# Expert rows of 8 KB with one gather per pick, and weights laid out load by load, in a two-block transformer kernel on one core

## What is computed

```
q       = h @ w_q                            # h: normed token, 1024 wide
scores  = q against two sets of 128 sub-keys, the best 16 sums kept per head
gate    = softmax over the 16 scores of a head
for each of the 128 picks e of a token:
    a   = gelu( sum_d h[d] * U[e, d] )       # U, V: 16384 rows of 1024 float32 per layer
    y  += gate * a * V[e, :]
x       = x + y
```

## Time and profile before

| | |
|---|---|
| median of 3 runs | 2161.14 us |
| span of the profiled execution | 2111.6 us |
| TensorE matmul busy | 1648.0 us (78%) |
| VectorE busy | 1375.4 us (65%) |
| ScalarE busy | 388.8 us (18%) |
| GpSimd busy (gathers) | 1128.4 us (53%) |
| moved by DMA | 720.79 MB, mean 341 GB/s |
| of that by GpSimd's queue, by SyncE's | 536.94 MB, 182.85 MB |

### The profile page before, as it was taken

How to read it: one execution, slowest core, us unless ns; L and a number is a source line. 1 busy time by engine, 2 the same in 40 slices (tenths; PEclk the granted TensorE clock), 3 DMA queues, 4 the chain that set the end, 5 groups by cost and what they waited for, 6 DMA issues and landing times.

```text
span 2111.6 us, 15758 instructions
## 1 busy us (share of the span) xinstructions
PE 1648.0 (78%) x4610; PEld 828.8 (39%) x4610; DVE 1375.4 (65%) x3269; ACT 388.8 (18%) x902; POOL 1128.4 (53%) x1028
## 2 busy tenths in 40 slices
PE   3997999998567978987876888878768996555565
PEld 1465887444233434432343433333434442111111
DVE  6564432142796695687757668776784887777775
ACT  1022000012121222222122222221322221100001
POOL 0000000000377577577766767776687777777773
PEclk9977999998789979999796999999788999887667
DMA  9851569162799999999999999999999999999997
GB/s 357 303 197 60 165 194 329 57 238 80 245 372 385 401 399 407 401 406 380 400 396 406 404 403 406 408 397 401 397 354 384 407 394 365 408 409 409 409 410 313
DMA packets 254483, 720.79 MB, mean 341 GB/s; under 512 B 24518, under 2 KB 49598, under 8 KB 253886
## 3 DMA queue, kind: packets, MB, share of 16 engines
q0 software_dynamic: 147456, 536.94, 65.0%
q1 hardware_dynamic: 106942, 182.85, 24.2%
HBM read 718.66 MB, written 1.05 MB: 341 GB/s over the span
## 4 chain that ended last, share of the span: by engine, by line
PE 40%; DMA 21%; POOL 17%; DVE 13%; issue 7%; ACT 2%; SPq 0%; POOLq 0%; DVEq 0%; ACTq 0%
POOL gring L1699 17%; DMA gring<-in_peer_v_dram,sel_idx 17%; PE PS L621 13%; PE PS L753 7%; PE PS L825 5%; PE PS L826 5%; DVE gring L1537 4%; PE PS L727 4%; PE PS L566 3%; DMA gring<-in_peer_u_dram,sel_idx 2%; DMA wring<-in_hyb_w_in_dram 1%; DVE xs L1556 1%; PE PS L670 1%; PE PS L687 1%; PE PS L706 1%
## 5 line engine op out<-in xcount | busy, mean ns | idle before, releaser
L1699 POOL DMA_INDIRECT gring<-in_peer_u_dram,sel_idx x512 | 566.0, 1105 | 725.1 <-DVE sel_g L1523 556.2
L825 PE MATMUL PS<-gring,diags 128*128 128x512 f32 x736 | 449.0, 695 | 321.3 <-DMA gring<-in_peer_v_dram,sel_idx 211.5
L1699 POOL DMA_INDIRECT gring<-in_peer_v_dram,sel_idx x512 | 562.2, 1098 | 230.3 <-issue 130.5
L1537 DVE CUSTOM_DVE_ANT_0 gring<-gring,hs 128x1024 f32<-128x1024 f32 x400 | 482.1, 1221 | 134.3 <-DMA gring<-in_peer_u_dram,sel_idx 133.1
L826 PE MATMUL PS<-gring,diags 128*128 128x512 f32 x736 | 434.2, 676 | 0.0
L621 PE MATMUL PS<-wring,hTs 128*128 128x512 f32 (+3 forms) x968 | 410.4, 574 | 9.8 <-DVE hTs L1125 4.3
L825 PEld LDWEIGHTS PS<-gring,diags 128*128 128x128 f32 x736 | 135.4, 210 | 545.4 <-issue 383.4
L621 PEld LDWEIGHTS PS<-wring,hTs 128*128 128x128 f32 x968 | 179.8, 195 | 219.8 <-issue 217.4
L826 PEld LDWEIGHTS PS<-gring,diags 128*128 128x128 f32 x736 | 158.8, 216 | 210.5 <-issue 210.5
L1063 ACT ACTIVATE diags<-consts,acts 128x128 f32<-128x128 f32 x368 | 136.4, 397 | 511.3 <-PE PS L826 476.8
L1537 DVE CUSTOM_DVE_ANT_0 gring<-gring,PS 128x1024 f32<-128x1024 f32 x112 | 136.4, 1220 | 70.4 <-DMA gring<-in_peer_u_dram,sel_idx 70.4
(11 more groups left out here) (194 smaller groups left out, 1188.9 us busy)
## 6 DMA issues: line engine op xcount, KB each, us to landing
wring<-in_peer_w_q_dram SPq DMA_DIRECT2D x32, 1024.0 KB, 14.7
wring<-in_w_ada_dram SPq DMA_DIRECT2D x24, 1024.0 KB, 9.7
wring<-in_w_up_dram SPq DMA_DIRECT2D x44, 512.0 KB, 5.1
wring<-in_hyb_w_in_dram SPq DMA_DIRECT2D x20, 1024.0 KB, 8.3
wring<-in_w_in_dram SPq DMA_DIRECT2D x10, 1024.0 KB, 8.1
wring<-in_hyb_w_out_dram SPq DMA_DIRECT2D x8, 1024.0 KB, 19.2
gring<-in_peer_u_dram,sel_idx POOLq DMA_INDIRECT x512, 12.9
gring<-in_peer_v_dram,sel_idx POOLq DMA_INDIRECT x512, 13.4
```

Source lines behind the costliest of these rows:

```text
L825: pe.e.matmul(ybank[0], d, row[i % NG][:, 0:512], start=first, stop=last)
L1537: e.tensor_tensor_reduce(row[i % NG], row[i % NG], hbank if (l, t) == (1, 1) and hd else h[t], 1.0, 0.0, ALU.mult, ALU.add, acts[:, c:c + ...
L1699: gp.e.indirect_dma_start(out=row[i % NG], out_offset=None, in_=table, in_offset=bass.IndirectOffsetOnAxis(ap=sel_idx[:, c:c + 1], axis=0) ...
```

## The change

- **Tables.** U and V of an expert stand side by side in one row of 8 KB (`peer_uv`, made on the host), and one gather per pick brings both: 512 gathers of 1 MB where there were 1024 of 512 KB. The slot is kept until the pick's sum or addition is done.
- **Rings.** `NG` is 11 slots of 8 KB (22 columns of 4 KB where there were 16), `NW` is 4 where it was 6. The three late gain vectors share one buffer, `late`, which is loaded three times, and some vectors of the first block move.
- **Order of expert steps.** The `v` step of a pick follows the `u` step of the pick two later (`LAG` = 2).
- **Gates pick by pick.** ScalarE applies Gelu to one column when its dot is done, and multiplies it with the gate (a Copy with scale); then, in the `v` step, it builds the diagonal of the pick two earlier, no longer ahead. VectorE's multiplication by the gates is gone.
- **Weights.** The host lays out each load as 128 runs of 8 KB. A load is one DMA of one run per partition (four runs for the narrow columns). The `up` loads are one DMA each where they were two of 512 KB; the sub-keys are laid out the same way.

```diff
-NG = 16
-NW = 6
+NG = 11
+NW = 4
+ROW = 2 * D
+LAG = 2
...
+    for n in range(len(picks) + LAG):
+        step = []
+        if n < len(picks):
+            if picks[n] == (1, 1, 1, 0):
+                step.append(("hold",))
+            step.append(("u", *picks[n]))
+        if n >= LAG:
+            step.append(("v", *picks[n - LAG]))
+        experts.append(step)
...
-    together(16 + 32 * 7, PACE[0], c00, hybrid(1), choose(1, 0))
+    together(16 * 8 - 4, PACE[0], c00, hybrid(1), choose(1, 0))
...
-                loads += [(("up", s[1], g), 2) for g in range(2)]
+                loads += [(("up", s[1], g), 1) for g in range(2)]
...
-            def gate(l, t, hd):
-                c0 = 128 * t + 16 * hd
-                ac.wait_ge(dotted, 16 * round_n[(l, t, hd)])
-                ac.e.activation(acts[:, c0:c0 + 16], acts[:, c0:c0 + 16], ACT.Gelu).then_inc(act_done, 1)
+            def gate(l, t, hd, j):
+                c = 128 * t + 16 * hd + j
+                n = dot_n[(l, t, hd, j)]
+                ac.wait_ge(dotted, n)
+                ac.e.activation(acts[:, c:c + 1], acts[:, c:c + 1], ACT.Gelu).then_inc(act_done, 1)
+                ac.wait_ge(chosen, chosen_n[(t, l, hd // 2)])
+                ac.wait_ge(act_done, n)
+                ac.e.activation(acts[:, c:c + 1], acts[:, c:c + 1], ACT.Copy,
+                                scale=sel_g[:, c:c + 1]).then_inc(weighted, 1)
...
-                ac.wait_ge(weighted, round_n[(l, t, hd)])
+                ac.wait_ge(weighted, dot_n[(l, t, hd, j)])
...
-                for col, w, r0, nk, c0, n in parts:
-                    src = w[r0:r0 + 128 * nk, c0:c0 + n].rearrange("(k p) n -> p k n", p=128)
-                    sp.e.dma_start(slot[s][:, 0:nk, col:col + n], src).then_inc(w_landed[s], 16)
+                w, at, nk, n = places[unit]
+                src = a[w][l, at:at + 128 * nk * n].rearrange("(p c) -> p c", p=128)
+                if n == 512:
+                    sp.e.dma_start(flat[s][:, 0:nk * n], src).then_inc(w_landed[s], 16)
...
-                sp.e.dma_start(kv, a["peer_sub_keys_2"][l].rearrange("h t n c -> n (h t) c")).then_inc(w_landed[s], 16)
+                sp.e.dma_start(kv, a["peer_sub_keys_2"][l]).then_inc(w_landed[s], 16)
...
-                gp.e.indirect_dma_start(out=row[i % NG], out_offset=None, in_=table,
+                gp.e.indirect_dma_start(out=gring[:, ROW * (i % NG):ROW * (i % NG + 1)], out_offset=None, in_=table,
                                         in_offset=bass.IndirectOffsetOnAxis(ap=sel_idx[:, c:c + 1], axis=0)
                                         ).then_inc(row_landed[i % NG], 16)
```

More of the change, by code:

```diff
@@ L228, in order @@
     left = []
+    picks = [(*r, j) for r in ROUNDS for j in range(16)]
     experts = []
-    waiting = []
-    for now, past in zip(ROUNDS + [None], [None] + ROUNDS):
-        if now == (1, 1, 1):
-            waiting = waiting + [("hold",)]
-        for j in range(16):
-            if now:
-                experts.append(waiting + [("u", *now, j)])
-                waiting = []
-            if past:
-                experts.append(waiting + [("v", *past, j)])
-                waiting = []
-        if now:
-            waiting = [("gate", *now)]
+    for n in range(len(picks) + LAG):
[7 more added lines that the diff above has]
+        experts.append(step)
     at = [0]
@@ L310, in program @@
         hTs = sb("hTs", 8 * 256)
-        gains = sb("gains", 3 * D)
+        late = sb("late", D)
         tabs = sb("tabs", 4 * 112)
@@ L362, in program @@
         hT = hTs[:, :].rearrange("p (k s) -> p k s", k=8)
-        late = [gains[:, D * i:D * (i + 1)] for i in range(3)]
         norm_cols = small[:, 368:392]
@@ L435, in program @@
         chosen_n = {key: n // 7 for key, n in chosen_n.items()}
-        gather_n = {s: n - 1 for s, n in counted(("u", "v")).items()}
-        gathers = [s for s in steps if s[0] in "uv"]
         dot_n = {s[1:]: n for s, n in counted(("u",)).items()}
+        picks = list(dot_n)
         sum_n = {s[1:]: n for n, s in enumerate((s for s in steps if s[0] == "v" and not by_vector(*s[1:])), 1)}
@@ L1569, in vector_engine @@
                    "angles": angles, "score": score, "value": value, "fold": fold, "up": up, "gfold": gfold,
-                   "index": index, "mrope": mrope, "hold": hold, "u": dot, "gate": gate, "v": expert, "pick": pick}
+                   "index": index, "mrope": mrope, "hold": hold, "u": dot, "v": expert, "pick": pick}
             first = {"mod": modulate, "turn": attturn, "lin": mrope_key}
@@ L1580, in sync_engine, with weights @@
             sp = Lane(eng)
-            def weights(key, parts):
+            places = unit_places()
+            def weights(key, unit, l=0):
                 s, _ = w_at[key]
@@ L1639, in up @@
                     for g in range(2):
[L1640 to L1646 removed]
+                        weights(("up", ch, g), ("up", ch, g))
             def down(t, c, k):
```

161 lines of the change are left out of this document (89 added, 72 removed).

## The result

The changed kernel takes 2304.12 us (median of 4 runs, 2302.51 to 2309.47), the kernel before 2156.47 in the runs beside it: a ratio of 1.0677, 95% interval 1.0635 to 1.072 (the ratios here are taken over all runs and differ by 0.1% or so from the quotient of two medians). On the three chips of the experiments the kernel before takes 2113 to 2118 us, and the changed one, run again on one of them, 2304.8, ratio 1.0896 (1.0866 to 1.0927). The changed kernel is slower by 7 to 9%. The prediction was 2147, about the same as before, with a range up to 2235: it was wrong in the direction and outside its range.

What follows compares the result with a forecast made beforehand. From about 557 us the DMA engines were taken as the bound, with compute engines waiting for rows. Steps 1 to 5, -90 + 46 + 16 + 12 + 2 = -14, gave 2097.6 us of span, scaled to 2147; range 2080 to 2235.

Steps and rivals of the forecast that it cites:

- Step 2: Attentions of the mixed stretch: sums wait behind the newest dot, a ring through three engines; +46 us, range 0 to 68.
- the absorption: Before each attention phase the slot ring runs empty, so 8 rows go in stock; 117 of 136 loads still move.
- the length of the ring: Score-to-score time through TensorE, VectorE and ScalarE: 9.5, 8.8, 7.1 or 3.6 us a unit, 335 us for three attentions.
- Step 1: Gathers and weights from 557 us on: 8 KB runs move at 425 GB/s, 1443 us where 1533 stood, -90 us.
- second rival: Gathers don't move faster in runs of 8 KB: only -43 us in step 1, 2195 us; chance 0.15.
- Step 3: First block's feed-forward: with four weight slots, second loads of chunks 2 to 5 stall TensorE; +16 us.
- Step 4: Windows where VectorE is nearly always busy, some 200 us, can't follow faster DMA: +12 us (0 to 25).
- third rival: The same ring closes in the selection of experts too: +68 us, 2217 us; chance 0.18.
- Step 5: End of the kernel: after the last row come a dot, Gelu, gate and addition; +2 us.
- The scaling: Forecast span of 2097.6 us times 2161.14 / 2111.6 = 1.0235, giving 2147 us for the runs.
- Slower by over 2%: Measured time over 2204 us: chance 0.23, of which 0.17 from the third rival and 0.06 from the second.

Runs made afterwards that it cites:

- mending the attentions alone: Changed kernel with ScalarE building the diagonal right behind its gate only for the 91 picks between units of the three mixed-stretch attentions: 2120.2 us, ratio 1.0022.
- the two kernels above: The changed kernel (2304.12 us), and the changed kernel with ScalarE building each pick's diagonal right behind its own gate (2080.96 us).
- the repaired kernel: Changed kernel with ScalarE building each pick's diagonal right behind its own Gelu and gate, not two picks later: 2080.96 us, ratio 0.9849.
- the fastest kernel: Changed kernel with each diagonal right behind its gate, plus six slots instead of four for the first block's weight loads: 2062.32 us, ratio 0.9739.

## Why the prediction was wrong

The forecast of the span was 2111.6 - 90 + 46 + 16 + 12 + 2 = 2097.6. It was 2300.7.

**Step 2, the lag of two picks: right mechanism, wrong size. This is the step that failed.** It said +46 us; the place of the diagonal costs 224, 185 of them through the attentions. Two parts of its working fell.

The first, and larger, is the absorption. "As the ring runs empty before each phase, 8 rows to put in stock" supposes that before each attention the engines wait for rows. They don't: between 577 and 1800 us of the changed kernel VectorE's waits are these (engine, tile and line, releaser: us in all, times, longest):

```profile
DVE work L1374 <- PE PS L710: 180.2, 41, 7.5
...
DVE gring L1574 <- DMA gring<-in_peer_uv_dram,sel_idx: 14.8, 11, 2.6
```

14.8 us for rows, 180.2 for scores behind sums. In the kernel before it is 131.2 us for rows of U, in 96 waits, and 33.2 for scores: the ring did run empty there, and the step carried that over. The slots are taken when the first attention begins, and GpSimd waits for one to be released (108.8 of the 188 us before the first attention, for sums): by the trace 58 gathers have been issued by 765 us, and 47 picks summed or added, eleven apart. A full ring can't take more rows in stock; each is issued when a sum ends, and while TensorE waits, none is. The argument took from the kernel before that its DMA share is 1.02 everywhere, and so that the DMA engines would still be the bound between the attentions. Once the sums wait for the newest dot there too, they are not. The right account for a ring that nothing drains is the time of the phase less what its own picks and weights need: by the prediction's own numbers 136 loads' time less 81 picks and 12 loads of weights, 43 x 2.47 = 106 us where it had 46. In the attention windows 164 were measured, and mending the attentions alone gave back 185.

The second is the length of the ring. 335 us were forecast for the 45 intervals and 362.7 measured (139.6, 102.8 and 120.4 for 128, 98 and 109). A unit with dot, addition, dot and sum was to take 8.8 us; the one shown takes 10.2. From the end of a score to the start of the next sum it is 0.7 (803.84 to the Exp at 804.53) + 4.85 (Exp to sum) = 5.5 us, where 4.7 + 1.0 was worked out. It is the sum that is longer: 799.18 to 802.97 us, 3.8 where 2.4 was put in, a mean over all granted clocks, with 2.9 as the slow end. A TensorE that waits nearly 5 us before each sum is granted a clock of 0.65 between 765 and 835 us, and its passes take 1.14 us instead of 0.592 (rows of the two kernels above), about twice as long, as at the lower of its two levels, 1.2 GHz. The wait makes the sum longer, and the sum the wait. The gates' 0.29 and the diagonal's 0.39 us for the 0.21 and 0.33 of the text are small beside it.

**Step 1, longer runs: the rate was right, the reason for it incomplete.** 421 GB/s in pure gathers where 425 was taken, and 421 in the attention windows of the repaired kernel. The prediction's second rival, that gathers don't move faster in 8 KB, falls. The Trainium skill, "DMA: Bandwidth & Descriptors", section "SWDGE vs HWDGE vs iDMA", says that a packet is preferably at most 4096 B; no loss by it shows in this trace, where rows of 8192 B, with half the packets, moved at 421 GB/s and rows of 4096 B at 410. What the step had wrong is "GpSimd is just ahead of them". It took the 0.94 us of one gather of the pure stretch for the mixed one, where the kernel with only its weights changed shows 1.16. So in the kernel before GpSimd and the DMA engines were about even, GpSimd issuing nearly without a pause (907 of 1024 gathers). That the weights' part is worth nothing (2118.69 for 2112.86) and that two gathers instead of one cost 56 us both fit that, and neither could be seen in a sum of bytes and rates. Of the -90 the fastest kernel keeps some 50: its gathers start at 558.8 us, within 3 us of before, and its span is 2063.0 for 2111.6.

**Step 3, a ring of four for the weights: right in place, near in size, and the size in part by luck.** Four idle times of TensorE at the line of `up`, ended by loads of `w_up`, were forecast with 16 us in all. They are there, with 2.2 to 3.1 us each and 11.4 in all. The first gather starts 21 us later (577.5 for 556.2), and undoing the ring of four gives back 19. What fills the gap was in no term: from 235 to 320 us, where the four waits lie, TensorE is granted a clock of 0.92 for 1.00 before, and its matmuls of `up` are busy 162.3 us in all, against 155.5 in the fastest kernel, with six slots:

```profile
PE PS L793 <- DMA wring<-in_w_up_dram: 11.4, 4, 3.1
POOL gring L1724 <- DVE sel_g L1559: 577.5, 1, 577.5
```

**Step 4, stretches that can't follow, and the third rival.** +12 us were put down. The windows between the attentions lose 85 us, and the repaired kernel loses next to nothing there (411 to 417 GB/s from 910 to 1640 us but for the attention). So it was no matter of a full VectorE: the same ring closes there too, as the third rival had it, "in the selection of experts too": VectorE waits 81.6 us for the matmuls of the key scores (L848) between 577 and 1800 us when only the attentions are repaired, and 45.0 when all is. But its share is small: 39 us of 224 are left when the attentions alone are repaired, against the 68 it was given. The attentions, in which the forecast itself lay, were sized at 46 and cost 185.

**Step 5** can't be told apart from the rest.

**The scaling.** 49.5 us between the span of the profiled execution and the median of the runs were carried over as a factor, 1.0235. The changed kernel's span and median differ by 3 us, and the kernel before takes 2113 to 2118 in the sets of the experiments, close to the span of its profile: the gap belongs to the first set of runs, whose four times scatter by 36 us (9 to 13 in the others), and not to every run. Why that set was slower stays open. Without the factor the forecast would have been 2098, still further off.

**The chances.** Slower by over 2% had 0.23 from mishaps elsewhere, none from step 2 itself. Of its bounds, 0 to 68, the upper varied the length of a sum alone; the absorption, on which more hung, had a bound only on the good side. Without the stock the same sum is -90 + 106 + 16 + 12 + 2 = +46, 2158 us of span, 2.2% over the time before: "slower" by the prediction's own numbers. It would still have been 143 us short of the 2300.7 measured; the longer sums of step 2 and the loss between the attentions are most of that.

## What to carry to other kernels

In an engine's queue an instruction waits for everything ahead of it: when a consumer is put n steps behind its producer, look at what stands in front of it in each queue, not only at n. Here, building the diagonal two picks late, behind the newest Gelu, cost 224 us, and doubling the distance changed nothing. Buffers absorb a slower phase only if something empties or fills them in between; ask which engine waits for the ring in the phase before, and if the producer already waits for a slot, count on nothing. A wait ahead of TensorE can be paid twice, as idle time and as a lower clock behind it: price the matmuls of a chain with waits by rows that have such waits. Price an issuing engine by the mean over the stretch that matters, since two rates within 5% of each other change places as soon as one moves.

## What the runs showed of the hardware

- A gather instruction of GpSimd takes 0.93 us in the pure stretch (150.87 / 162) and 1.16 in the mixed one (891.11 / 766), 0.93 to 2.0 us for single ones. In the pure stretch VectorE's dots read their second operand from PSUM, in the mixed one mostly both from SBUF. Set side by side in time, the rows of the kernel before part by that: between 600 and 1800 us, 261 gathers during which VectorE ran no dot or addition on rows in SBUF took 0.945 us on average, and 375 that overlapped a dot with both operands in SBUF 1.24; after 1800 us 162 gathers that overlapped a dot with one operand in PSUM took 0.937. The Trainium skill, "GPSIMD Engine Reference", section "1. Specifications", says that GpSimd's SBUF interfaces are shared with VectorE and contend with its instructions of two SBUF inputs; the trace agrees, though no run here changed the dots alone.
- In the pure stretches 8 KB rows gathered by GpSimd move at 421 GB/s, 4 KB rows at 410. There the gathers of the kernel before land 11.0 us after their issue, so they are queued and the rate is that of the DMA engines. The window of the kernel with two gathers a pick has 400, with most of its slices at 408 to 410.
- A pass of a float32 matmul of 128x512 takes 0.592 us on a TensorE that is kept busy and 1.06 to 1.22 us where it waits nearly 5 us between sums (granted clock 0.93 and 0.65).
- ScalarE is busy 720 us where it was 389, through gates of one column and table loads of 1.283 us each. Leaving the Gelu out, and 132 of the 157 table loads with it, gives back 29 us in the changed kernel and nothing clear of noise in the fastest one.
